# The low halves of the first query, key and value weight tiles made by GpSimd instead of VectorE

## What is computed

```python
mod_lat = (silu_c @ ada_w[i] + ada_b[i])[:, None, :]
u_lat = modulate(rms_norm(h_lat, g_mix[i]), sh1, sc1)
w = na_wqkv[j]
ql, kl, vl = jnp.split((u_lat @ w).reshape(B, L, 3, H, dh), 3, axis=2)
ql, qc = rms_norm(ql, na_q_gain[j]), rms_norm(qc, na_q_gain[j])
y_lat = neighborhood_attention(ql, kl, vl, kc, vc, na_rpb[j]) @ na_wo[j]
```

## Time and profile before

| | |
|---|---|
| median of 3 runs | 1671.03 us (1670.35 to 1674.38) |
| profiled execution | 1670.41 us |
| its span, first to last instruction | 1668.6 us |
| TensorE busy | 1595.2 us (96%) |
| VectorE busy | 1285.8 us (77%) |
| ScalarE busy | 862.1 us (52%) |
| GpSimd busy | 114.0 us (7%) |
| `w_lo` on VectorE, line 1777 | 372 instructions, 452.3 us |

### The profile page before, as it was taken

One profiled execution on the slowest core, in us unless ns is written; L12 is line 12 of the kernel. 1 busy time (PEld: TensorE's weight loads), 2 busy tenths in 40 slices (PEclk: granted clock), 3 DMA queues, 4 the chain that ended last, 5 costly groups with the idle time before them and its releaser, 6 DMA issues.

```text
span 1668.6 us, 32386 instructions
## 1 busy us (share of the span) xinstructions
PE 1595.2 (96%) x11866; PEld 1417.7 (85%) x11866; DVE 1285.8 (77%) x2209; ACT 862.1 (52%) x1484; POOL 114.0 (7%) x194
## 2 busy tenths in 40 slices
PE   6999999799999999799899999789999999999999
PEld 5778767588888888686799999689999999799999
DVE  6899886888767877679678787777887687588874
ACT  4664585343223433457565555255555577565552
POOL 0001120000000014140001112000000000000000
PEclk8999999899999999999999999989999999999999
DMA  9246651445667855360356668735555555065554
GB/s 372 97 150 230 215 140 41 149 144 184 202 200 229 262 201 150 118 179 6 125 157 209 216 197 288 286 102 175 178 183 189 196 161 163 22 199 179 186 189 139
DMA packets 81598, 292.25 MB, mean 175 GB/s; under 512 B 10816, under 2 KB 12864, under 8 KB 79568
## 3 DMA queue, kind: packets, MB, share of 16 engines
q1 hardware_dynamic: 69680, 249.09, 45.8%
q0 software_dynamic: 11808, 41.68, 7.7%
HBM read 270.74 MB, written 18.68 MB: 173 GB/s over the span
## 4 chain that ended last, share of the span: by engine, by line
PE 75%; DVE 15%; ACT 3%; issue 3%; DMA 3%; SPq 0%; DVEq 0%; ACTq 0%
PE bank L787 23%; PE bank L788 22%; PE bank L789 22%; DVE w_lo L1777 2%; DVE prob L2435 1%; DVE bank L2417 1%; DMA raw<-weights 1%; DVE bank L1789 1%; DVE stat L2423 1%; DVE ada_raw L1790 1%; PE bank L887 1%; PE bank L1040 1%; DMA ada_first<-ada_w 1%; PE bank L1023 1%; DVE bank L2412 1%
## 5 line engine op out<-in xcount | busy, mean ns | idle before, releaser
L787 PE MATMUL bank<-u_hi,w_hi 128*128 128x256 f32 (+1 forms) x1936 | 614.7, 318 | 28.0 <-DVE u_lo L2241 19.1
L788 PE MATMUL bank<-u_lo,w_hi 128*128 128x256 f32 (+1 forms) x1936 | 601.8, 311 | 0.0
L789 PE MATMUL bank<-u_hi,w_lo 128*128 128x256 f32 (+1 forms) x1936 | 601.4, 311 | 0.0
L1777 DVE TENSOR_TENSOR w_lo<-raw,w_hi 128x1024 fp32r<-128x1024 f32 x372 | 452.3, 1221 | 132.1 <-ACT w_hi L1293 119.9
L1293 ACT ACTIVATE w_hi<-raw 128x1024 fp32r<-128x1024 f32 x360 | 376.3, 1052 | 191.5 <-PE bank L789 157.6
L787 PEld LDWEIGHTS bank<-u_hi,w_hi 128*128 128x128 f32 x1936 | 373.5, 193 | 57.8 <-issue 36.0
L788 PEld LDWEIGHTS bank<-u_lo,w_hi 128*128 128x128 f32 x1936 | 373.5, 193 | 22.1 <-issue 3.8
L789 PEld LDWEIGHTS bank<-u_hi,w_lo 128*128 128x128 f32 x1936 | 373.4, 193 | 18.7
L787 PE MATMUL bank<-hid_hi,w_hi 128*128 128x512 f32 (+1 forms) x512 | 174.1, 340 | 0.0
L789 PE MATMUL bank<-hid_hi,w_lo 128*128 128x512 f32 (+1 forms) x512 | 172.1, 336 | 0.0
L788 PE MATMUL bank<-hid_lo,w_hi 128*128 128x512 f32 (+1 forms) x512 | 172.0, 336 | 0.0
(11 more groups left out here) (341 smaller groups left out, 2226.2 us busy)
## 6 DMA issues: line engine op xcount, KB each, us to landing
raw<-weights SPq DMA_DIRECT2D x372, 512.0 KB, 3.6
ada_raw<-ada_w SPq DMA_DIRECT2D x80, 512.0 KB, 4.3
ada_first<-ada_w SPq DMA_DIRECT2D x16, 512.0 KB, 13.8
bias_sb<-bias_na POOLq DMA_DIRECT2D x16, 256.0 KB, 3.3
toep_dram<-zeros POOLq DMA_DIRECT2D x8, 512.0 KB, 9.0
bat_dram<-bat POOLq DMA_DIRECT2D x16, 256.0 KB, 4.2
ca_dram<-ca POOLq DMA_DIRECT2D x16, 256.0 KB, 3.6
s_bat<-bat_dram POOLq DMA_DIRECT2D x4, 1024.0 KB, 10.1
```

Source lines behind the costliest of these rows:

```text
L787: pe.matmul(dst, wh, hi[:, kt, xs], start=first, stop=False)
L788: pe.matmul(dst, wh, lo[:, kt, xs], start=False, stop=False)
L789: return pe.matmul(dst, wl, hi[:, kt, xs], start=False, stop=final)
L1777: TT(w_lo[:, slot, :], raw[:, slot, :], w_hi[:, slot, :].bitcast(F32), ALU.subtract).then_inc(S["lo"], 1)
```

## The change

Units 3 to 23 (`LOWER_BY_POOL`) get their low halves from GpSimd, in the same form and by the same count. VectorE's `lower` returns at once for them; before unit 24 it waits until `lo` shows that all earlier ones are done. GpSimd makes units 3 to 15 ahead of its two table stores, 16 to 19 behind the load of the constants, and 20 to 23 behind the first four bias loads and ahead of the store `rot_dram`. Its first one waits until VectorE has made unit 2.

```diff
+        LOWER_BY_POOL = range(3, ST["v0"].unit0 + ST["v0"].tiles)
...
+                if isinstance(i, int):
+                    g = i * per + g_static
+                    if g in LOWER_BY_POOL:
+                        return
+                    if g == LOWER_BY_POOL[-1] + 1:
+                        dve.wait_ge(S["lo"], CREDIT + g)
                 dve.wait_ge(S["hi"], i * per + (CREDIT + g_static + 1))
                 TT(w_lo[:, slot, :], raw[:, slot, :], w_hi[:, slot, :].bitcast(F32), ALU.subtract).then_inc(S["lo"], 1)
...
+            def lower(g):
+
+                pool.wait_ge(S["hi"], CREDIT + g + 1)
+                if g == LOWER_BY_POOL[0]:
+                    pool.wait_ge(S["lo"], CREDIT + g)
+                slot = g % RING
+                pool.tensor_tensor(w_lo[:, slot, :], raw[:, slot, :], w_hi[:, slot, :].bitcast(F32), ALU.subtract).then_inc(S["lo"], 1)
+
+            late = ST["qk0"].tiles
+            for g in LOWER_BY_POOL:
+                if g < late:
+                    lower(g)
             pool.wait_ge(pre_e, 4)
             pool.wait_ge(pre_v, 4)
             pool.dma_start(pw_dram, pw[:, 0:2]).then_inc(pre_saved, 16)
             pool.dma_start(bbar_dram, bbar[:, :, :, :]).then_inc(pre_saved, 16)
             pool.wait_ge(S["unit"], CREDIT + 2)
             pool.dma_start(con[:, N_EARLY:], cons[:, N_EARLY:]).then_inc(late_in, 16)
+            for g in LOWER_BY_POOL:
+                if late <= g < late + 4:
+                    lower(g)
...
                 if b == 4:
+                    for g in LOWER_BY_POOL:
+                        if g >= late + 4:
+                            lower(g)
                     pool.wait_ge(pre_v, 5)
                     pool.dma_start(rot_dram, rot0[:, :, :, :]).then_inc(rot_saved, 16)
```

## The result

The changed kernel takes 1691.19 us as the median of 4 runs (1689.7 to 1694.12), beside 1670.69 us for the kernel before on the same chip. The medians differ by 20.5 us. The ratio on record is 1.0132, with a 95% interval of 1.0117 to 1.0148 (the quotient of the two medians is 1.0123): slower, clear of noise. The forecast was 1678, its range ended at 1687. The direction was right, the size was not.

A forecast was written before the change was run, and what follows sets the result against it. VectorE's gapless row ahead of `v0` was taken to bound its start. Terms 7.3 + 2 - 0.8 = +8.5 us, less 0.5, made +8 on the profiled 1670.41: 1678 us, range 1667.5 to 1687.

The forecast's parts named there:

- What bounds the stretch: Ahead of `v0`, a 48.7 us row of VectorE work sets its start; changes show at TensorE above 1.58 us slack.
- The duration: Each of GpSimd's 21 subtractions of 1024 columns takes two passes, 2.1 us, between bounds of 1.1 and 3.1 us.
- The full hold: VectorE stands still for the whole of each GpSimd subtraction, 2.1 us; this case or near it had chance 0.50.
- Rivals 1 and 2: Beside GpSimd's subtractions: no hold, 1668.0 us, chance 0.14; partial hold or short operation, 1668 to 1675 us, chance 0.27.
- 3 and 4: Slow GpSimd operations, 1682 us and up, chance 0.09; TensorE waiting for GpSimd's low halves in `v0`, part of that.
- rows 8: Trace rows where VectorE's scaling pair takes 1.19 instead of 0.88 us while GpSimd issues eight stores; read as a hold.
- Let line 2045 alone run beside it: VectorE's line 2045, one input from PSUM, isn't held; two of eight subtractions fall on it, 1.5 us less.
- The row ahead of `v0`: Between 93.70 and 142.45: eight subtractions add 16.8 us, 8.0 go out, 1.5 less for line 2045: +7.3 us.
- Between 61 and 94 us: Six GpSimd operations put in 12.6 us and take out 6.8; +3.2 us after gaps, of which 2 counted.
- 0.8 us of gains: TensorE's shorter waits at unit 3 and at the attention remain as gains, 0.8 us taken off the sum.
- 0.5 for room: Some 0.5 us taken off the sum of +8.5 us for tiles whose step has room.
- `v0`: the step that failed: In `v0`, GpSimd's five operations (10.5 us) replace VectorE's five (5.7) and meet its 4.11 us DMA wait: nothing added.

The follow-up runs named there:

- the copy: The changed kernel with each of GpSimd's 21 subtractions replaced by a copy of `raw` into `w_lo` (one SBUF input): 1668.69 us, ratio 0.9997.
- the memset: The changed kernel with each of GpSimd's 21 subtractions replaced by a memset of `w_lo` (nothing read): 1667.29 us, ratio 0.9979.
- the split run: The changed kernel with each GpSimd subtraction cut into four of 256 columns, each waiting for the one before: 1688.27 us, ratio 1.0119.

## Why the prediction was right, and where it was wrong

**What bounds the stretch: right.** "What is added to or taken from that row shows at TensorE." Both directions held: 52 subtractions added there cost 20.6 us, the same ones in a stage with room cost nothing, and one product taken out of the row's way took away the wait of 1.58 us (the gain in time, 1.35 us, is not clear of noise).

**The duration: right, a little short.** Taken as two passes, 2.1 us; it is 2.39 us alone and 2.55 in the mean, as it also waits for VectorE. The hold is 2.18 us each. That two inputs pass one after the other was the author's estimate, with no row behind it. The runs give the durations alone: 1024 columns take 0.96 us with nothing read, 1.04 with one input, 2.39 with two.

**The full hold: right.** It was inferred from a different pair of instructions; the copy (0.76 us of hold) and the memset (none) show that it goes with what GpSimd reads. Rivals 1 and 2, no hold and a partial one, fall, and so do 3 and 4: the first subtraction takes 2.39 us, the longest 3.39, and no wait of TensorE is put down to GpSimd. That the premise led to the right hold was in part luck, as none of the instructions in rows 8 has two SBUF inputs. The stores' 925 ns against 538, read as GpSimd being held, bear little weight: in the run with the subtractions ahead of them they take 884 ns each at 520 us, beside other work of VectorE. "Let line 2045 alone run beside it": right too, though no row of before showed it. Its 16 instances take 751 ns in the mean, as before.

**The row ahead of `v0`: mechanism right, sum too small by a third.** From the row at 93.70 to line 2045 of tile 13 it took 48.0 us; the same instructions take 57.1 now, from 96.42 to 153.50. Eight subtractions fall in it, as counted, and seven low halves went out (8.0 us): 17.1 us of hold, 2.14 each, where 16.8 less 1.5 were booked. The term that was too small is the duration: eight times 2.39 us are 19.1, and the 2.0 us by which the holds stay under that are near the discount of 1.5 for line 2045. How they are saved is another matter: line 2045 runs free, but the next instruction with two inputs waits for the rest. Between 61 and 94 us the row came out 2.7 us later, not 2. And 0.8 us of gains plus 0.5 for room were taken off, of which nothing is left at `v0`'s start. The row stands at 153.50 instead of 141.70, 11.8 us later, where it was forecast at about 150; `v0` starts 11.8 us later.

**`v0`: the step that failed.** "In `v0` GpSimd's five operations (10.5 us) replace VectorE's five (5.7 us) and meet its 4.11 us of waiting for a DMA, so nothing is added there." From VectorE's first instruction behind tile 15 to line 2412 of the attention it was 37.4 us before (151.67 to 189.08), and is 42.7 now (166.53 to 209.27, now line 2420). Four subtractions lie in it, 9.8 us of hold, 2.46 each (with the 1.0 us that line 2337 stood ahead of them), and 5.7 us went out. The waits for a DMA took up none of it; they grew by 1.0 us, from 4.11 to 4.76 and 0.36:

```profile
191.31 0.33 SPq L603 DMA_DIRECT2D ada_raw<-ada_w  x1
```

```profile
191.20 0.08 DVE L1798 DVE_READ_ACCUMULATOR ada_raw<-ada_raw,silu_row 128x1 f32 x1
198.78 1.23 DVE L1797 SCALAR_TENSOR_TENSOR bank<-ada_raw,silu_row 128x1024 f32<-128x1024 f32 x1 [4.76 <-DMA ada_raw<-ada_w]
209.27 0.69 DVE L2420 TENSOR_TENSOR bank<-bank,bias_sb 128x512 f32<-128x512 f32 x1
```

`ada_raw` has two slots. SyncE issues this load only when VectorE has read the product two before it, at 191.28, and the product that needs it starts 7.5 us later. Before, the same load was issued at 171.08 and the product behind it ran at 178.59: 7.5 us as well. The load is tied to VectorE's own progress, so a VectorE that is late gets its data late by as much, and the idle time stays. It could have taken up only what falls between that issue and that landing, and no subtraction does. The rest of the lag is in front: behind tile 15 VectorE is 14.9 us late, 3.1 more than at tile 13; 1.75 of it is the hold of unit 19 on that tile's line 2055. The other 1.3 us are TensorE's: VectorE waits 5.56 us at 162.66 for the root of tile 15, which waits for TensorE, and TensorE's lag grows from 11.8 to 13.1 us behind the wait at 154.62, while the granted clock is low.

So the loss is 11.8 us up to `v0` (9.3 forecast from the row, 8 after deductions) and 8.4 in it (none forecast): 20.2. The 8.4 are the holds of five subtractions less the five low halves that went out, 5.9 us, the 1.0 us more of waiting for a DMA, and the 1.3 us of the clock, all but 0.2. As forecast, no low half was late for TensorE, the wait for unit 3's was gone, and GpSimd's moved stores and loads cost nothing (the store `rot_dram` was issued at 189.03, not at about 172, since VectorE's table was late, and still in time).

**Left out altogether:** the clock. Each of the waits of 2.71, 5.36 and 7.31 us was followed by some us at a lower granted clock (0.51, 0.72 and 0.56 in the stretches above), which cost 3.1, 1.3 and 2.7 us more. The prediction booked a wait at its length. The 3.1 us ahead of `v0` are hidden, as VectorE's row sets `v0`'s start: they only made the wait there shorter. The 1.3 us are counted in the 8.4, and the last 2.7 us take the lag from 20.2 to 22.2 us, as some short waits of before are gone there.

A slip of the text: `v0` has 8 modulation products, not the 7 that stand in the description of the kernel before.

**The range** ended at 1687 since the price of `v0` was zero in all its cases. The same sum with `v0`'s five operations booked at what they add, 10.5 - 5.7 = 4.8 us, gives 1683; with 2.39 for 2.1 us in those five and the eight ahead of `v0`, 1687; and without the deductions of 0.8 and 0.5 us, 1688. The profiled execution took 1690.25.

## What to carry to other kernels

Where VectorE has no gap, work moved from it to GpSimd pays only if GpSimd's instruction holds VectorE for less than VectorE saves. Here it was 2.18 us of hold for 1.14 saved with two inputs read, 0.76 with one, none with a memset. Look for the move's price first in the stretch where VectorE has no gap: the same 52 subtractions cost 20.6 us there, and nothing where it had 27 us of room in 80. An idle gap of the held engine takes up a delay only if what ends the gap doesn't itself wait for that engine (here the product ran 7.5 us after the issue that waits for VectorE, before and after, and the gap was 4.11 us, then 4.76); find the issue of the transfer that ends it before booking anything against it.

## What the runs showed of the hardware that was not expected

- GpSimd's instructions stretch as well: its 256-column subtractions took 1315 ns in the mean beside VectorE's products of 1024 columns in the later stage, 1036 ns in `qk0`. The two wait for each other, instruction by instruction.
- Two GpSimd subtractions directly behind each other let one VectorE instruction through between them in two cases of the changed kernel (73.47 and 100.31) and none in the third (one of 0.69 us took 6.37, and had started while GpSimd issued loads). Where GpSimd waited on a semaphore between its quarters, VectorE got its turn as well, as the rows of the split run show.
- Eight stores of 512 KB moved by 296 us made VectorE wait 11 us more for its loads and the kernel 4.3 us slower (with the stores in their place the same subtractions cost nothing), while the same number of bytes moved.
